# Gated feed-forward with gate and up columns in every chunk and the weights stationary

## The chip, the cores and the metric

One core of a Trainium2 chip runs the whole program. The metric is the device time of one launch in microseconds (us).

## The reference, cut to what matters

A token block of 256 rows with 1024 features goes through ten sublayers of two models, one behind the other. Four of them are gated feed-forwards (before and after each of the two mixers of the first model):

```python
def swiglu(x, w_gu, w_down):
    g, u = jnp.split(x @ w_gu, 2, axis=-1)
    return (jax.nn.silu(g) * u) @ w_down
...
x = layer_norm(ALPHA * x + 0.5 * swiglu(x, ffn_w_gu[l, 0], ffn_w_down[l, 0]), ln_g[l, 0], ln_b[l, 0])
```

`w_gu` is 1024 x 5632 (2816 gate columns, then 2816 up columns) and `w_down` 2816 x 1024, all float32. The second model has two feed-forwards without a gate, `square(relu(h @ w_up)) @ w_down`, with `w_up` 1024 x 4096.

## The kernel before, in words

**Stages and linears.** The program is a list of ten stages, and each is written once for each engine. A gated feed-forward is a stage of kind `ffn1` (four of them: the first, the third, the fourth and the sixth stage), an ungated one `ffn2`. A `Linear` is cut into chunks of CH = 512 output columns, and a chunk into blocks of 256 rows of the contraction (two tiles of 128). The up linear of `ffn1` has 11 chunks of 4 blocks, the down linear 2 chunks of 11 blocks.

**Weights.** SP loads each block (512 KB) into one of 8 `raw` slots (L621). Products are made of float32 numbers split into a high and a low part: ACT copies the block to `whi` (L744, in `split`), DVE subtracts and writes `wlo` (L1285, in `rest`), into one of 4 slots. A slot is free for block b when PE has used block b - 4 (`block_used`).

**Two forms of product.** In the token form (`rows`, L2264 to L2266) the input's tile of 128 tokens is stationary and 512 weight columns stream past it: 3 matmuls of 512 columns for each contraction tile and each half of the tokens, 48 for a chunk. The result has tokens on the partitions. In the paired form (`paired`, L2451, L2452 and L2454) a tile of 128 x 128 weights is stationary; the input's high and low parts lie side by side, so the high weights take one matmul of 512 columns and the low weights one of 256. A chunk has 32 of each, and its result has features on the partitions. It fills all four `stream` banks, each of which holds two halves that must still be added: ACT copies the first half (`copy_halves`, L765), DVE adds the second (`add_halves`, L1296). The token form fills two banks, so that it alternates between two pairs. Paired chunks were in use for chunks 1 to 7 of `ffn2` and for five chunks of each `hg` mixer.

**The gated stage.** All 11 chunks of the up linear are in the token form. Chunks 0 to 4 are gate columns, which ACT evicts with Silu to `silu_gate` (L755); chunk 5 is half gate, half up; chunks 6 to 10 are up columns, which ACT copies to `up_part`. DVE multiplies (`product`, L1534). The down linear needs h with its features on the partitions, so that PE turns h by 44 transposes in a stage (`h_turn`, L2311, first argument `const`): 4 behind chunk 6, 8 behind each of chunks 7 to 10 and 8 inside the down linear. Each turned bank is split by ACT (`hhi`, L792) and DVE (`hlo`, L1321).

**What sets the order.** Each engine runs its own list in program order; they meet at semaphores alone. `evicted` tells PE that `stream` banks are free. A paired chunk starts with the banks that the chunk before did not use last, and waits for the other two ahead of its third output tile:

```python
if at.like - 1 not in lin.paired:
    order = [(j, m) for half in ((0, 1), (2, 3)) for j in range(SPLIT - 2) for m in half]
...
if (j, m) == (0, 2):
    pe.wait_ge(evicted, 2 * lin.chunk(at))
```

The first condition holds for the first paired chunk of a linear: it does eight pairs of matmuls before it needs the other banks, where the later ones do four. Chunk 0 is done by `first_rows` in the later stages (L2293 to L2302) and by `rows` in the first.

## Time and profile before

| | |
|---|---|
| median of 3 runs | 1906.47 us (1905.2 to 1908.08) |
| profiled execution | 1904.79 us, its span 1903.0 us |
| PE busy | 1873.5 us, 98% |
| DVE busy | 1291.4 us, 68% |
| ACT busy | 972.5 us, 51% |
| moved by the DMA queues | 342.47 MB, 180 GB/s |

Matmul records overlap, so that the cost of one is read from the distance between starts and not from its duration. A row of a timeline has the start, the duration, the engine, the line and the operation; "x8" merges eight records, and brackets tell idle time before it and who ended that. PE is TensorE, PEld its weight loads, ACT ScalarE, DVE VectorE.

### The profile page before, as it was taken

What the parts mean: (1) busy time and instruction counts of PE and PEld (TensorE: products, weight loads), DVE (VectorE), ACT (ScalarE), POOL (GpSimd) and SP (SyncE); (2) the same over time, 40 slices, a digit from 0 to 9 for tenths busy, and PEclk for the clock granted to TensorE, in tenths of its full rate; (3) what the DMA queues carried; (4) which work ended last, traced back from release to release, by engine and by line L of the source; (5) the groups of instructions that cost most, each with busy time, mean ns of one, the idle gap of its engine ahead of it and who ended that gap; (6) DMA issues with size and microseconds to landing.
All of it is one profiled execution on the core that took longest, in us unless ns stands there. A gap on an engine that the chain in (4) does not pass through costs nothing.

```text
span 1903.0 us, 25523 instructions
## 1 busy us (share of the span) xinstructions
PE 1873.5 (98%) x9697; PEld 1592.3 (84%) x9697; DVE 1291.4 (68%) x1670; ACT 972.5 (51%) x1266; POOL 36.0 (2%) x67
## 2 busy tenths in 40 slices
PE   9999989999999999999989999999999999999998
PEld 7888877888888888788879888888888988888887
DVE  4565877465646678845576997687656798777754
ACT  5454564454445456545446446455544644555543
POOL 1010100000000000000000000000000000000000
PEclk9999999999999999999999999999999999999999
DMA  9666536665666665576545554466565554455662
GB/s 319 192 197 217 193 110 191 189 183 182 209 191 184 181 186 145 164 216 184 185 146 183 183 181 129 139 197 187 190 192 185 183 173 162 131 172 182 188 196 81
DMA packets 173578, 342.47 MB, mean 180 GB/s; under 512 B 10976, under 2 KB 11152, under 8 KB 173344
## 3 DMA queue, kind: packets, MB, share of 16 engines
q1 hardware_dynamic: 169360, 327.26, 55.3%
q0 software_dynamic: 4112, 13.77, 2.2%
q8 instruction: 70, 1.15, 0.2%
q14 instruction: 36, 0.29, 0.0%
HBM read 338.36 MB, written 1.05 MB: 178 GB/s over the span
## 4 chain that ended last, share of the span: by engine, by line
PE 82%; DVE 14%; ACT 2%; issue 1%; DMA 0%; SPq 0%; DVEq 0%; ACTq 0%
PE stream L2264 18%; PE stream L2266 17%; PE stream L2265 17%; PE stream L2451 6%; DVE wlo L1285 4%; PE stream L2452 3%; PE aux L2311 3%; PE stream L2431 2%; PE stream L2433 2%; PE stream L2432 2%; PE stream L2302 1%; PE stream L2293 1%; PE stream L2294 1%; PE stream L2370 1%; PE stream L2371 1%
## 5 line engine op out<-in xcount | busy, mean ns | idle before, releaser
L1285 DVE TENSOR_TENSOR wlo<-raw,whi 128x1024 fp32r<-128x1024 f32 x584 | 706.4, 1223 | 480.3 <-ACT whi L744 477.6
L744 ACT ACTIVATE whi<-raw 128x1024 fp32r<-128x1024 f32 x584 | 609.3, 1057 | 534.9 <-PE stream L2266 426.1
L2264 PE MATMUL stream<-whi,x_split 128*128 128x512 f32 x944 | 372.7, 395 | 2.7 <-DVE wlo L1285 2.7
L2266 PE MATMUL stream<-whi,x_split 128*128 128x512 f32 x944 | 368.1, 390 | 0.0
L2265 PE MATMUL stream<-wlo,x_split 128*128 128x512 f32 x944 | 367.5, 389 | 0.0
L2264 PE MATMUL stream<-whi,hhi 128*128 128x512 f32 x672 | 263.3, 392 | 0.0
L2266 PE MATMUL stream<-whi,hlo 128*128 128x512 f32 x672 | 261.6, 389 | 0.0
L2265 PE MATMUL stream<-wlo,hhi 128*128 128x512 f32 x672 | 261.5, 389 | 0.0
L2451 PE MATMUL stream<-x_split,whi 128*128 128x512 f32 x672 | 241.0, 398 | 0.0
L2264 PEld LDWEIGHTS stream<-whi,x_split 128*128 128x128 f32 x944 | 177.3, 188 | 38.4 <-issue 3.3
L2266 PEld LDWEIGHTS stream<-whi,x_split 128*128 128x128 f32 x944 | 177.2, 188 | 37.7
L2265 PEld LDWEIGHTS stream<-wlo,x_split 128*128 128x128 f32 x944 | 177.5, 188 | 35.3
L2452 PE MATMUL stream<-x_split,wlo 128*128 128x256 f32 x768 | 199.2, 280 | 0.0
L2452 PEld LDWEIGHTS stream<-x_split,wlo 128*128 128x128 f32 x768 | 144.7, 188 | 8.3
L2451 PEld LDWEIGHTS stream<-x_split,whi 128*128 128x128 f32 x672 | 126.3, 188 | 26.6 <-ACT relu_part L755 0.4
L2266 PEld LDWEIGHTS stream<-whi,hlo 128*128 128x128 f32 x672 | 126.1, 188 | 26.4
L2265 PEld LDWEIGHTS stream<-wlo,hhi 128*128 128x128 f32 x672 | 126.2, 188 | 25.5
L2264 PEld LDWEIGHTS stream<-whi,hhi 128*128 128x128 f32 x672 | 126.2, 188 | 25.4
L2431 PE MATMUL stream<-x_split,whi 128*128 128x256 f32 x416 | 118.8, 286 | 0.0
L2432 PE MATMUL stream<-x_split,whi 128*128 128x256 f32 x416 | 117.7, 283 | 0.0
L2433 PE MATMUL stream<-x_split,wlo 128*128 128x256 f32 x416 | 117.7, 283 | 0.0
L2432 PEld LDWEIGHTS stream<-x_split,whi 128*128 128x128 f32 x416 | 79.8, 192 | 0.3
(345 smaller groups left out, 2091.0 us busy)
## 6 DMA issues: line engine op xcount, KB each, us to landing
raw<-ffn_w_gu SPq DMA_DIRECT2D x176, 512.0 KB, 4.3
raw<-w_in SPq DMA_DIRECT2D x136, 512.0 KB, 4.6
raw<-ffn_w_down SPq DMA_DIRECT2D x88, 512.0 KB, 3.8
raw<-w_up SPq DMA_DIRECT2D x64, 512.0 KB, 4.3
raw<-w_down SPq DMA_DIRECT2D x64, 512.0 KB, 4.4
raw<-c_w_in SPq DMA_DIRECT2D x24, 512.0 KB, 3.8
raw<-ab_w_in SPq DMA_DIRECT2D x20, 512.0 KB, 5.2
raw<-w_out SPq DMA_DIRECT2D x16, 512.0 KB, 3.7
```

The costliest lines, as they stand in the source:

```text
L744: act.activation(split_slots(lin, at, j)[0], raw[:, b % RAW], ACT.Copy).then_inc(hi_ready, 1)
L1285: dve.tensor_tensor(lo, raw[:, b % RAW], hi.bitcast(F32), ALU.subtract).then_inc(lo_ready, 1)
L2264: pe.matmul(bank[tt][:], hi, wh, start=kt == 0, stop=False)
L2265: pe.matmul(bank[tt][:], hi, wl, start=False, stop=False)
L2266: mm = pe.matmul(bank[tt][:], lo, wh, start=False, stop=kt == last)
L2293: pe.matmul(bank[:], hi, wh[:, k], start=(j, k) == (0, 0), stop=False)
L2311: t = pe.transpose(bank[:, m * P:(m + 1) * P], src[:, bass.ds(first + m * P, P)], ident)
L2431: pe.matmul(to, wh, xhi[:, kt, tokens], start=first, stop=False, skip_group_check=True)
L2432: pe.matmul(to, wh, xlo[:, kt, tokens], start=False, stop=False, skip_group_check=True)
L2433: mm = pe.matmul(to, wl, xhi[:, kt, tokens], start=False, stop=last, skip_group_check=True)
L2451: pe.matmul(banks[m], wh[:, k], both, start=kt == 0, stop=False)
L2452: mm = pe.matmul(banks[m][:, S:CH], wl[:, k], xhi[:, kt], start=False, stop=False)
```

## The change

Every chunk c of the up linear now holds gate columns 256c to 256c + 255 and the up columns of the same numbers, so that each is whole: its h can be made at once. A block comes by two transfers of 256 KB, whose rows are 1 KB and not 2 KB (`transfers`). Chunk 0 stays in the token form, chunks 1 to 10 become paired. Output tiles 0 and 1 of a chunk are the gate, 2 and 3 the up half. For each paired chunk ACT applies Silu in place in `h_part` (`gate`), DVE multiplies (`product`), and ACT and DVE split the product straight into `hhi` and `hlo` (`h_hi`, `h_lo`), with no transpose. Only the h of chunk 0 is turned, by 4 transposes into one bank behind chunk 1. The arrays `silu_gate`, `up_part` and `relu_part` give way to two buffers `h_part`, which `ffn2` uses too.

```diff
@@ -164,7 +162,7 @@
         for i in range(2):
-            up = Linear(io["ffn_w_gu"][l, i], D, 2 * D_FF)
+            up = Linear(io["ffn_w_gu"][l, i], D, 2 * D_FF, paired=range(1, 11), sides=2)
             down = Linear(io["ffn_w_down"][l, i], D_FF, D)
...
@@ -270,6 +268,15 @@
         return self.w[j * BK * P:(j + 1) * BK * P, self.columns(at)]
+
+    def transfers(self, slot, at, j):
+
+        if self.sides == 1:
+            return [(slot, self.source(at, j).rearrange("(k p) n -> p k n", p=P))]
+        n, rows = CH // self.sides, slice(j * BK * P, (j + 1) * BK * P)
+        return [(slot[:, :, i * n:(i + 1) * n],
+                 self.w[rows, bass.ds(at.c * n + i * self.w.shape[1] // self.sides, n)]
+                 .rearrange("(k p) n -> p k n", p=P)) for i in range(self.sides)]
 
     def columns(self, at):
         return bass.ds((self.order[at.like] if at.like < len(self.order) else at.c) * CH, CH)
...
@@ -350,10 +357,7 @@
 
-        silu_gate = sb("silu_gate", [P, TT, FF1], at=56 * KB)
-        up_part = [sb(f"up_part{i}", [P, TT, CH], at=56 * KB + TT * FF1 * 4 + i * 4 * KB) for i in range(2)]
-
-        relu_part = [sb(f"relu_part{i}", [P, TT, CH], at=(64 + 4 * i) * KB) for i in range(2)]
...
@@ -552,6 +561,11 @@
 
+        transfers_of = [lin.sides for lin in lins for _ in range(lin.n * lin.kb)]
+
+        def landed(b):
+            return 16 * sum(transfers_of[b % RAW:b + 1:RAW])
+
...
@@ -617,8 +631,8 @@
-                    src = lin.source(at, j)
-                    sp.dma_start(raw[:, slot], src.rearrange("(k p) n -> p k n", p=P)).then_inc(raw_in[slot], 16)
+                    for to, src in lin.transfers(raw[:, slot], at, j):
+                        sp.dma_start(to, src).then_inc(raw_in[slot], 16)
...
@@ -886,36 +900,56 @@
 
             def ffn1(st):
                 up, down = st.lins
-                split(up, At(0), SPLIT)
+                h0, l0 = seen.h, gated_before(st)
+                a0 = seen.aux
 
                 def gate(at):
-                    split(up, At(at.like + 1, at.turn))
-                    evict(up, at, lambda tt: silu_gate[:, tt, bass.ds(at.c * CH, CH)], ACT.Silu)
-
-                chunks(act, 0, 5, gate, peel=1)
-                split(up, At(6))
-                act.wait_ge(block_used, up.done(At(5)))
+
+                    act.wait_ge(evicted, 2 * up.chunk(at) + 2)
+                    tiles = part_tiles(at)(0, 2)
+                    act.activation(tiles, tiles, ACT.Silu).then_inc(gate_made, 1)
+
+                def h_hi(at):
+
+                    act.wait_ge(h_made, h0 + at.c + 1)
+                    act.activation(hhi[:, bass.ds(2 * at.c, 2), :], part_tiles(at)(0, 2), ACT.Copy).then_inc(gated_hi, 1)
+
+                def body(at, to=up):
+
+                    before = At(at.like - 1, at.turn)
+                    split(up, at, 2, 3)
+                    gate(before)
+                    split(up, at, 3, 4)
+                    h_hi(before)
+                    split(to, At(at.like + 1, at.turn) if to is up else At(0), 0, 2)
+                    if at.like > 2:
+
+                        act.wait_ge(gated_lo, l0 + at.c - 2)
+                    copy_halves(up, at, part_tiles(at))
+
+                split(up, At(1))
+                act.wait_ge(block_used, up.done(At(0)))
                 for tt in range(TT):
-                    bank = stream[up.banks(At(5)) + tt]
-                    act.activation(silu_gate[:, tt, 5 * CH:FF1], bank[:, 0:CH // 2], ACT.Silu)
-                    act.activation(up_part[1][:, tt, CH // 2:CH], bank[:, CH // 2:CH], ACT.Copy).then_inc(evicted, 1)
-                h0 = seen.h
-                for c in range(6, up.n):
-                    if c + 1 < up.n:
-                        split(up, At(c + 1))
-                    else:
-                        ahead(down)
-                    if c > 6:
-
-                        act.wait_ge(h_made, h0 + c - 6)
-                    evict(up, At(c), lambda tt: up_part[c % 2][:, tt, :])
-                    if c == PARAMS_CHUNK and st is stages[0]:
-                        seen.aux += 1
-                    h_turn_hi(*FF1_TILES[c - 1])
+                    bank = stream[up.banks(At(0)) + tt]
+                    act.activation(h_part[0][:, tt, 0:S], bank[:, 0:S], ACT.Silu)
+                    act.activation(h_part[0][:, tt, S:CH], bank[:, S:CH], ACT.Copy).then_inc(evicted, 1)
+                split(up, At(2), 0, 2)
+                copy_halves(up, At(1), part_tiles(At(1)))
+                turn_hi(by_tokens(hhi), 4)
+
+                act.wait_ge(aux_full, a0 + 1)
+                body(At(2))
+                chunks(act, 3, up.n - 1, body)
+                if st is stages[0]:
+                    seen.aux += 1
+                body(At(up.n - 1), down)
+                split(down, At(0), 2, 3)
+                gate(At(up.n - 1))
+                split(down, At(0), 3, 4)
+                h_hi(At(up.n - 1))
                 split(down, At(0), SPLIT, SPLIT + 2)
-                h_turn_hi(*FF1_TILES[up.n - 1])
                 last_layer(down, SPLIT + 2)
-                seen.h += 6
+                seen.h = h0 + up.n
...
@@ -1522,31 +1556,49 @@
 
                 up, down = st.lins
-                chunks(dve, 1, 7, lambda at: rest(up, at), peel=1)
-
-                def product(c):
-
-                    cols = slice(CH // 2, CH) if c == 5 else slice(0, CH)
-                    at = c * CH + cols.start - FF1
-                    dve.wait_ge(evicted, 2 * (up.c0 + c) + 2)
-                    part = silu_gate[:, :, at:at + cols.stop - cols.start]
-                    dve.tensor_tensor(part, part, up_part[c % 2][:, :, cols], ALU.mult).then_inc(h_made, 1)
-
-                product(5)
-                for c in range(6, up.n):
-                    if c + 1 < up.n:
-                        rest(up, At(c + 1))
-                    else:
-                        ahead(down)
-                    product(c)
-                    if c == PARAMS_CHUNK and st is stages[0]:
-                        copy_params()
-
-                        dve.wait_ge(const_in, 32)
-                    h_turn_lo(*FF1_TILES[c - 1])
+                l0 = gated_before(st)
+
+                def product(at):
+
+                    dve.wait_ge(gate_made, l0 + at.c)
+                    part = part_tiles(at)
+                    dve.tensor_tensor(part(0, 2), part(0, 2), part(2, 4), ALU.mult).then_inc(h_made, 1)
+
+                def h_lo(at):
+
+                    dve.wait_ge(gated_hi, l0 + at.c)
+                    tiles = bass.ds(2 * at.c, 2)
+                    dve.tensor_tensor(hlo[:, tiles, :], part_tiles(at)(0, 2), hhi[:, tiles, :].bitcast(F32),
+                                      ALU.subtract).then_inc(gated_lo, 1)
+
+                def body(at, to=up):
+
+                    before = At(at.like - 1, at.turn)
+                    rest(up, at, 2, 3)
+                    product(before)
+                    rest(up, at, 3, 4)
+                    h_lo(before)
+                    rest(to, At(at.like + 1, at.turn) if to is up else At(0), 0, 2)
+                    add_halves(up, at, part_tiles(at))
+
+                rest(up, At(1))
+                dve.wait_ge(evicted, 2 * up.c0 + 2)
+                part = h_part[0][:]
+                dve.tensor_tensor(part[:, :, 0:S], part[:, :, 0:S], part[:, :, S:CH], ALU.mult).then_inc(h_made, 1)
+                rest(up, At(2), 0, 2)
+                add_halves(up, At(1), part_tiles(At(1)))
+                turn_lo(by_tokens(hhi), by_tokens(hlo), 4)
+                chunks(dve, 2, up.n - 1, body)
+                if st is stages[0]:
+                    copy_params()
+
+                    dve.wait_ge(const_in, 32)
+                body(At(up.n - 1), down)
+                rest(down, At(0), 2, 3)
+                product(At(up.n - 1))
+                rest(down, At(0), 3, 4)
+                h_lo(At(up.n - 1))
                 rest(down, At(0), SPLIT, SPLIT + 2)
-                h_turn_lo(*FF1_TILES[up.n - 1])
                 last_layer(st, SPLIT + 2)
...
@@ -2512,18 +2558,21 @@
                     first_rows(up)
                 else:
                     rows(up, At(0), xhi, xlo, ready=x_ready())
-                chunks(pe, 1, 7, lambda at: rows(up, at, xhi, xlo), peel=1)
-                h0 = seen.h
-                a0 = seen.aux + (st is stages[0])
-                for c in range(6, up.n):
-                    if c > 6:
-                        rows(up, At(c), xhi, xlo)
-                    if c == PARAMS_CHUNK and st is stages[0]:
-                        turn_params()
-                    h_turn(c - 1, h0)
-                last_layer(st, hhi, hlo, ready=lambda j, tt: (aux_free, a0 + 2 + 2 * ((j + 1) // 2)),
-                           hook=lambda j: h_turn(up.n - 1, h0) if j == 2 else None)
-                seen.h += 6
+                paired(up, At(1))
+                h0, a0, l0 = seen.h, seen.aux, gated_before(st)
+                pe.wait_ge(h_made, h0 + 1)
+                bank = aux_bank()
+                for a in range(2):
+                    for tt in range(TT):
+                        t = pe.transpose(bank[:, (2 * a + tt) * P:(2 * a + tt + 1) * P],
+                                         h_part[0][:, tt, a * P:(a + 1) * P], ident)
+                t.then_inc(aux_full, 1)
+                chunks(pe, 2, up.n - 1, lambda at: paired(up, at))
+                if st is stages[0]:
+                    turn_params()
+                paired(up, At(up.n - 1))
+                last_layer(st, hhi, hlo, ready=lambda j, tt: (gated_lo, l0 + j) if j else (aux_free, a0 + 1))
+                seen.h = h0 + up.n
```

**ACT, chunk 0 and what comes behind it.** In the rows below, from ACT's list in the first gated stage, `h_part_69` and `h_part_70` are the two buffers of `h_part`. Before:

```order
L744 ACTIVATE whi<-raw 128x1024 [waits block_used,raw_in7]
L755 ACT_TABLE_LOAD
L755 ACTIVATE silu_gate<-stream 128x512 [waits block_used]
L755 ACTIVATE silu_gate<-stream 128x512
L246 UNCONDITIONAL_BRANCH
```

Now:

```order
L758 ACTIVATE whi<-raw 128x1024 [waits block_used,raw_in7]
L934 ACT_TABLE_LOAD
L934 ACTIVATE h_part_69<-stream 128x256 [waits block_used]
L935 ACTIVATE h_part_69<-stream 128x256
L934 ACTIVATE h_part_69<-stream 128x256
L935 ACTIVATE h_part_69<-stream 128x256
L758 ACTIVATE whi<-raw 128x1024 [waits block_used,raw_in0]
L758 ACTIVATE whi<-raw 128x1024 [waits block_used,raw_in1]
L779 ACTIVATE h_part_70<-stream 128x512 [waits tiles_full]
```

The eviction of chunk 0 is four instructions in place of two, behind the same table load and the same four splits of chunk 1.

**PE, from chunk 0 to its eviction's wait.** Before, chunk 1 was in the token form in the two free banks, and the first instruction that waited for the eviction of chunk 0 stood at the start of chunk 2:

```order
L2265 MATMUL stream<-wlo,x_split 128x512
L2266 MATMUL stream<-whi,x_split 128x512
L246 UNCONDITIONAL_BRANCH
L246 ISA
L2256 ISA [waits evicted]
L2264 MATMUL stream<-whi,x_split 128x512 [waits lo_ready]
```

Now, inside chunk 1 (the first row with a wait is the ninth of its pairs of matmuls):

```order
L2498 MATMUL stream<-x_split,wlo 128x256
L2497 MATMUL stream<-x_split,whi 128x512 [waits evicted]
L2498 MATMUL stream<-x_split,wlo 128x256
L2497 MATMUL stream<-x_split,whi 128x512
L2498 MATMUL stream<-x_split,wlo 128x256
```

The wait has moved up by a chunk less eight pairs.

**ACT, a late chunk of the first gated stage.** Before, while PE did chunk 6:

```order
L744 ACTIVATE whi<-raw 128x1024 [waits block_used,raw_in7]
L755 ACTIVATE up_part_70<-stream 128x512 [waits block_used]
L755 ACTIVATE up_part_70<-stream 128x512
L792 ACTIVATE hhi<-aux 128x2x128 [waits aux_full] x2
L744 ACTIVATE whi<-raw 128x1024 [waits block_used,raw_in0]
```

Now, chunk 9 (`L779` is `copy_halves`, `L910` the gate and `L915` `h_hi` of the chunk before):

```order
L758 ACTIVATE whi<-raw 128x1024 [waits block_used,raw_in6]
L910 ACTIVATE h_part_69<-h_part_69 128x512 [waits evicted]
L758 ACTIVATE whi<-raw 128x1024 [waits block_used,raw_in7]
L915 ACTIVATE hhi<-h_part_69 128x512 [waits h_made]
L758 ACTIVATE whi<-raw 128x1024 [waits block_used,raw_in0]
L758 ACTIVATE whi<-raw 128x1024 [waits block_used,raw_in1]
L779 ACTIVATE h_part_70<-stream 128x512 [waits tiles_full,gated_lo]
L779 ACTIVATE h_part_70<-stream 128x256 [waits tiles_full]
L779 ACTIVATE h_part_70<-stream 128x256 [waits block_used]
```

Silu and the high part of h, each of 512 elements, now stand between the splits.

## Rows read from the trace of the kernel before

**Rows 1.** Page, busy time of the engines and the granted clock.
```profile
PE 1873.5 (98%) x9697; PEld 1592.3 (84%) x9697; DVE 1291.4 (68%) x1670; ACT 972.5 (51%) x1266; POOL 36.0 (2%) x67
...
PEclk9999999999999999999999999999999999999999
```

**Rows 2.** Waits of PE, the matmul that waited longest.
```profile
PE stream L2264 <- DVE wlo L1285: 2.7, 2, 2.5
```

**Rows 3.** Groups by line and shape: busy us, mean ns | idle before.
```profile
L2264 PE MATMUL stream<-whi,x_split 128*128 128x512 f32 x944 | 372.7, 395 | 2.7 <-DVE wlo L1285 2.7
...
L2452 PE MATMUL stream<-x_split,wlo 128*128 128x256 f32 x768 | 199.2, 280 | 0.0
...
L2311 PE MATMUL aux<-const,silu_gate 128*128 128x128 f32 x176 | 23.2, 273 | 0.0
```

**Rows 4.** Timeline of ACT, second gated stage (start us, us, what).
```profile
328.49 1.07 ACT L755 ACTIVATE silu_gate<-stream 128x512 f32 x2
...
339.37 1.07 ACT L755 ACTIVATE silu_gate<-stream 128x512 f32 x2
...
417.88 1.07 ACT L755 ACTIVATE up_part<-stream 128x512 f32<-128x512 f32 x2
...
429.65 1.07 ACT L755 ACTIVATE up_part<-stream 128x512 f32<-128x512 f32 x2
```

**Rows 5.** Timeline of PE, second gated stage, ends of its chunks 1 to 10.
```profile
316.44 0.39 PE L2264 MATMUL stream<-whi,x_split 128*128 128x512 f32 x1
...
429.22 0.47 PE L2264 MATMUL stream<-whi,hhi 128*128 128x512 f32 x1
```

**Rows 6.** Timeline of PE, the first stage with paired chunks alone.
```profile
1274.88 0.39 PE L2451 MATMUL stream<-x_split,whi 128*128 128x512 f32 x1
...
1277.72 0.49 PE L2451 MATMUL stream<-x_split,whi 128*128 128x512 f32 x1
...
1286.21 1.04 PE L2311 MATMUL aux<-const,relu_part 128*128 128x128 f32 x8
...
1354.61 0.40 PE L2264 MATMUL stream<-whi,hhi 128*128 128x512 f32 x1
```

**Rows 7.** Timelines of ACT, DVE and PE in that stage.
```profile
1276.60 1.07 ACT L755 ACTIVATE relu_part<-stream 128x512 f32<-128x512 f32 x2
...
1309.72 0.38 ACT L765 ACTIVATE relu_part<-stream 128x256 f32<-128x256 f32 x1 [1.03 <-PE stream L2454]
...
1320.99 0.38 ACT L765 ACTIVATE relu_part<-stream 128x256 f32<-128x256 f32 x1 [1.03 <-PE stream L2454]
...
1310.14 0.42 DVE L1296 TENSOR_TENSOR relu_part<-stream,relu_part 128x256 f32<-128x256 f32 x1 [0.98 <-ACT relu_part L765]
...
1310.93 0.40 PE L2451 MATMUL stream<-x_split,whi 128*128 128x512 f32 x1
```

**Rows 8.** Timeline of ACT and PE, chunk 0 of gated stages 2 and 1.
```profile
318.28 1.28 ACT L755 ACT_TABLE_LOAD   x1
...
319.57 1.09 ACT L755 ACTIVATE silu_gate<-stream 128x512 f32<-128x512 f32 x2
...
22.96 1.28 ACT L755 ACT_TABLE_LOAD   x1
...
24.25 1.09 ACT L755 ACTIVATE silu_gate<-stream 128x512 f32<-128x512 f32 x2
...
21.62 0.39 PE L2264 MATMUL stream<-whi,x_split 128*128 128x512 f32 x1
```

**Rows 9.** Timeline of ACT, two evictions of 256 columns each.
```profile
383.91 0.66 ACT L792 ACTIVATE hhi<-aux 128x256 fp32r<-128x256 f32 x2
```

**Rows 10.** DMA queues of the page, and a window of the first stage.
```profile
q1 hardware_dynamic: 169360, 327.26, 55.3%
...
q0 software_dynamic: 4112, 13.77, 2.2%
...
20.00:86.00 66.00, 66.00 (x293) 54.62 (x293) 30.49 (x26) 32.92 (x40) 0.00 (x0) 1.00 0.76 237
```

More of the change, by code:

```diff
@@ L40 @@
 RAW = 8
-PARAMS_CHUNK = 8
 SPLIT = 4
@@ L112 @@
 FF1 = D_FF
-FF1_TILES = {5: (0, 2)} | {c: (2 + 4 * (c - 6), 4) for c in range(6, 11)}
 PARAM_ROWS = 64
@@ L254, with __init__ @@
 class Linear:
-    def __init__(self, w, k, n, order=(), walk=None, paired=()):
-        self.order, self.walk, self.paired = order, walk, paired
+    def __init__(self, w, k, n, order=(), walk=None, paired=(), sides=1):
+        self.order, self.walk, self.paired, self.sides = order, walk, paired, sides
         self.w, self.kb, self.n = w, k // (P * BK), n // CH
@@ L351, in program @@
         hlo = sb("hlo", [P, 32, S], F32R, at=32 * KB)
-        silu_gate = sb("silu_gate", [P, TT, FF1], at=56 * KB)
-        up_part = [sb(f"up_part{i}", [P, TT, CH], at=56 * KB + TT * FF1 * 4 + i * 4 * KB) for i in range(2)]
-        relu_part = [sb(f"relu_part{i}", [P, TT, CH], at=(64 + 4 * i) * KB) for i in range(2)]
+        h_part = [sb(f"h_part{i}", [P, TT, CH], at=(64 + 4 * i) * KB) for i in range(2)]
         y = sb("y", [P, TT, D], at=72 * KB)
@@ L446, in program @@
         tiles_from = lambda dst, first: lambda a, b: dst[:, first + a:first + b, :]
-        relu_tiles = lambda at: lambda a, b: relu_part[at.like % 2][:].rearrange("p a (b t) -> p (a b) t", b=2)[:, a:b]
+        part_tiles = lambda at: lambda a, b: h_part[at.like % 2][:].rearrange("p a (b t) -> p (a b) t", b=2)[:, a:b]
+        by_tokens = lambda t: t[:, 0:2].rearrange("p a (h t) -> p (a h) t", h=2)
+        gated_before = lambda st: (st.lins[0].n - 1) * [s for s in stages if s.kind == "ffn1"].index(st)
         raw_in = [sem(f"raw_in{i}") for i in range(RAW)]
@@ L1211, in halves @@
                 def halves(at):
-                    copy_halves(up, at, relu_tiles(at))
+                    copy_halves(up, at, part_tiles(at))
                 def h_hi(at):
@@ L1217, in h_hi @@
                     act.activation(hhi[:, bass.ds(4 * at.c, 4), :],
-                                   relu_part[at.like % 2][:].rearrange("p a (b t) -> p (a b) t", b=2), ACT.Copy)\
+                                   h_part[at.like % 2][:].rearrange("p a (b t) -> p (a b) t", b=2), ACT.Copy)\
                         .then_inc(h_hi_ready, 1)
@@ L1222, in ffn2 @@
                 split(up, At(1))
-                evict(up, At(0), lambda i: relu_part[0][:, i, :], ACT.Relu)
+                evict(up, At(0), lambda i: h_part[0][:, i, :], ACT.Relu)
                 split(up, At(2), 0, 2)
@@ L2163, in square @@
                     dve.wait_ge(evicted, 2 * up.chunk(at) + 2)
-                    part = relu_part[at.like % 2][:]
+                    part = h_part[at.like % 2][:]
                     dve.scalar_tensor_tensor(part, part, 0.0, part, ALU.max, ALU.mult).then_inc(h_made, 1)
@@ L2395, in walked @@
                 seen.x_src, seen.x_early = [src], True
-            def h_turn(c, h0):
-                first_tile, tiles = FF1_TILES[c]
-                pe.wait_ge(h_made, h0 + c - 4)
-                for tt in range(TT):
-                    turn(silu_gate[:, tt], first_tile * P, tiles)
             def columns(lin, at, ready=None, hook=None):
@@ L2827, in ffn2 @@
                 for tt in range(TT):
-                    turn(relu_part[0][:, tt], 0, 4)
+                    turn(h_part[0][:, tt], 0, 4)
                 chunks(pe, 2, up.n, lambda at: paired(up, at))
```

16 lines of the change are left out of this document (9 added, 7 removed).

## The prediction

> **What bounds the kernel now.** I read the page first: PE is busy 98% of the span, and its granted clock is full in all forty slices, the 2.4 GHz level [rows 1]. Then the waits of PE: the longest total for a `stream` matmul is 2.7 us in 1903 [rows 2]. So the sum of what PE issues is the time, and ACT, DVE and the DMA queues count only where they make PE wait. Then the groups, for the shapes [rows 3], and the timelines, for distances between starts, since a record of a matmul lasts longer than what it costs. I compare the gated stages as they are with the first `ffn2` stage, which is the only place where nothing but paired chunks run one behind the other.
>
> **PE in a gated stage now.** ACT evicts at the end of each chunk, so its evictions tell the period of a chunk: 339.37 - 328.49 = 10.88 us for a token chunk without a turn, and 429.65 - 417.88 = 11.77 us with 8 transposes [rows 4]. A turn of 8 costs 0.89 us, 0.11 us for each, and one of 4 half of it, 0.45 us. From the start of chunk 1 to the end of chunk 10 and its turn it is 429.22 - 316.44 = 112.78 us [rows 5], which agrees with 10 x 10.88 + 0.45 + 4 x 0.89 = 112.8. The last turn, in the down linear, adds 0.89. Together 113.67 us a stage.
>
> **PE in a gated stage after it.** Chunk 1 is the first paired one: 1286.21 - 1274.88 = 11.33 us [rows 6], with a pause of 0.1 us inside. Chunks 2 to 7 with a turn of 8 take 1354.61 - 1286.21 = 68.40 us [rows 6]; here the turn has 4 transposes, so that 0.45 goes off: 67.95. Chunks 8 to 10 take 1320.99 - 1309.72 = 11.27 us each [rows 7], 33.81. The sum is 113.09 us: 0.58 less than 113.67. In four stages **-2.3 us**. So 40 fewer transposes give 4.5 us a stage, and ten chunks that cost 0.39 us more each give 3.9 of it back. Both forms stream 24576 columns for a chunk (48 x 512, or 32 x 512 + 32 x 256), but the paired form needs 64 matmuls and weight loads for what the token form does with 48.
>
> Here a rule of the Trainium skill would say otherwise. The page "TensorE: Matmul & The Clock Gate" (Wait — 56ns, not 53.3ns?) puts a warm matmul at its columns over 2.4 GHz plus a fixed 2.5 ns or so. By it, as an estimate, sixteen more matmuls cost a chunk 0.04 us and not 0.39, and the change would give some 16 us more. The trace doesn't agree: 48 matmuls take 10.88 us, 227 ns each, and the page's sum would be 10.4 us.
>
> **The wait that is added.** Chunk 1 needs the banks of chunk 0 at its ninth pair. In `ffn2` PE comes to it 1277.72 - 1274.88 = 2.84 us behind the start of chunk 1 [rows 6]; there ACT began the eviction 1276.60 - 1274.88 = 1.72 us behind that start and took 1.07 [rows 7], so it ended at 2.79: just in time. In a gated stage ACT must first load the table that has Silu. That load starts when the splits of chunk 1 are done, at 318.28, and the eviction at 319.57 [rows 8]: 3.13 us behind the start of chunk 1 at 316.44 [rows 5]. Today nobody waits for it, since chunk 1 has banks of its own. The eviction is then four instructions of 256 columns; two such take 0.66 us [rows 9], one 0.385 (the third `copy_halves` shows 0.38 [rows 7]), so each further one adds 0.275: 0.385 + 3 x 0.275 = 1.21 us. End at 4.34, 1.55 us later than in `ffn2`, where PE was just held. PE stands still for some 1.55 us in each of the three later gated stages, 4.65 us. In the first stage chunk 1 starts at 21.62 and the eviction at 24.25 [rows 8], 2.63 us behind; with 1.21 that is 3.84, 1.05 us more than 2.79. Together **+5.7 us**. Bounds: 0, if PE's order had more slack than in `ffn2`, and 4 x 1.28 more, if the table load repeated.
>
> A second rule speaks against the change. The page "ScalarE: Activation LUTs" (What ACT_TABLE_LOAD costs) adds a drain of about 1.38 us to a table load of 1.28. With it, as an estimate, the four pauses would cost 5.5 us more. The rows show the load from 318.28 to 319.56 and the eviction at 319.57, so no drain stands there, and the sum goes by the rows.
>
> **The start.** Blocks come by two transfers with rows of half the size. The trace has no packets of 1 KB in number. Queue 1 moved 169360 packets in 55.3% of 16 engines' span, 99 ns for each of 1.93 KB; queue 0 moved 4112 in 2.2%, 163 ns for each of 3.35 KB [rows 10]. The difference is 45 ns a KB and leaves 12 ns for a packet whatever its size. An engine has 16 packets more in a block, 0.2 us. PE's second block waits for the landing of the first two, **+0.4 us** once (0 if bytes alone count, 3.2 us if a packet of 1 KB costs 99 ns). Later it is covered: the queues are busy 0.76 in the heaviest stretch of the first stage [rows 10], and 12 ns on 99 make it 0.85. SP issues twice as much, with eight blocks of lead.
>
> **What is hidden.** ACT's splits, copies, Silu and high part make about 7 us in a chunk of 11.27, and DVE's four blocks of 1.22, the product, the low part and the adds about 8. The tightest meeting is that of the third add with the fifth pair of the next chunk: in `ffn2` the add ends at 1310.14 + 0.42 = 1310.56 and PE comes at 1310.93 [rows 7], 0.37 us later. Silu and `h_hi` stand behind this add in ACT's list, and in both lists between splits that PE needs 5.6 us on, so they are costed at nothing. If one came ahead of it, PE would wait in each chunk.
>
> **The sum.** -2.3 + 5.7 + 0.4 = +3.8 us on the profiled execution's 1904.79 us, or 1908.6. The median of the runs is 1.7 us above that execution, so that I put the median after at 1906.47 + 3.8 = **1910.3 us**. Something like 0.2% (3.8 us) is what a measurement of this kernel can tell from no change, and the forecast lies on that line.
>
> **Rivals.**
> - *Each pair runs at its quicker rate.* Behind the turn in `ffn2` chunk 2 took 68.40 - 0.89 - 5 x 11.27 = 11.16 us, 0.11 less than its followers. If all nine and chunk 1 had that or somewhat better (0.16), 5 us go: 1905. Against it: all five later chunks of `ffn2` took 11.27. Chance 0.13.
> - *PE isn't held in chunk 1*, if the eviction ends in time after all: 1910.3 - 5.7 = 1904.6. For it only that ffn2's margin is not seen exactly. Chance 0.08.
> - *A matmul costs its columns*, half a 512-column one for 256, so that a pair takes 340 ns and a chunk 10.88 us: 40 x 0.39 = 15.6 us less, 1895, a faster kernel. The fixed 2.5 ns of the Trainium skill's page on TensorE would lead there. Against it: 32 pairs in 11.27 us are 352 ns. Chance 0.04.
> - *The other side: a wait in every chunk.* `copy_halves` or its add comes a split late (1.06 us on ACT), because ACT or DVE is held by the new exchange of Silu, product and the two parts of h. It decides from 0.37 us of delay on; 1.06 - 0.37 = 0.69 us in 36 chunks is 25 us: 1935. Against it: each piece of the exchange has 2 us or more before PE's next need. Chance 0.08.
> - *The queues become the bound*, if a packet of 1 KB costs as one of 2 KB: 0.76 would become 1.5, more than there is, and the up linears would take half as long again. Chance 0.02.
>
> **How the numbers follow.** The forecast has 0.65, with a range of its own from 1908 to 1913, about half of it on either side of the line. Faster by over 0.2%: the column case and a little of the rest, 0.07. Within: half of the forecast and the two mild rivals, 0.49. Slower: the other half and the two severe cases, 0.44. The range of 1904 to 1916 leaves out the column case, the severe ones and a small edge.
>
> **What would show it.** Right: chunks 3 to 10 at 11.27 us by ACT's third copies; a PE pause of 1.5 us inside chunk 1 of three stages, 1 us in the first, ended by ACT's line 935; 16 transposes of h in all; no drain behind the table load; the first stage's second block landing some 0.4 us later. Wrong: a pause of PE in the steady chunks, a chunk nearer 10.9 or 11.1, or DMA as the releaser of ACT's splits in the up linear.

## The result, and the profile after

The changed kernel takes 1911.93 us (median of 7 runs, 1910.67 to 1918.22) against 1905.90 (7 runs, 1905.2 to 1908.08): a ratio of 1.0031, 95% interval 1.0021 to 1.0041. It is slower by some 6.0 us. 1910.3 was forecast.

The profiled execution took 1912.12 us with a span of 1910.5, 7.5 more than the span before. The page of the changed kernel, busy time by engine, the granted clock and the first queue:

```profile
PE 1873.3 (98%) x10177; PEld 1608.8 (84%) x10177; DVE 1349.9 (71%) x1806; ACT 1002.3 (52%) x1342; POOL 35.8 (2%) x67
PEclk9999999999999999999999999999999999999999
q1 hardware_dynamic: 217232, 327.27, 54.2%
```

PE is the bound as before [rows 1]. Queue 1 moves the same bytes in 47872 more packets, and its share of the span did not rise (55.3% before, [rows 10]). The waits of PE (line, releaser; us in total, times, longest):

```profile
PE stream L2497 <- ACT h_part L935: 5.7, 4, 1.4
PE stream L2316 <- DVE wlo L1319: 4.2, 1, 4.2
```

The first row is new: four pauses, one in each gated stage, ended by the eviction of chunk 0. The second answers to [rows 2], where it was 2.7 us: the wait for the very first block.

The second gated stage on PE: the start of chunk 1, the last two matmuls ahead of the pause and the first behind it, the turn of 4, and the start of the down linear:

```profile
320.79 0.39 PE L2497 MATMUL stream<-x_split,whi 128*128 128x512 f32 x1
...
323.25 0.40 PE L2497 MATMUL stream<-x_split,whi 128*128 128x512 f32 x1
323.48 0.28 PE L2498 MATMUL stream<-x_split,wlo 128*128 128x256 f32 x1
325.18 0.50 PE L2497 MATMUL stream<-x_split,whi 128*128 128x512 f32 x1 [1.42 <-ACT h_part L935]
...
333.73 0.60 PE L2567 MATMUL aux<-const,h_part 128*128 128x128 f32 x4
...
435.66 0.40 PE L2316 MATMUL stream<-whi,hhi 128*128 128x512 f32 x1
```

From 320.79 to 435.66 it is 114.87 us, where 113.67 were worked out for the stage before (1.20 more; 0.97 more was forecast). The third stage has 114.84 and the fourth 114.85, read the same way, the first 115.23. In the 113.67 the last turn, which stood inside the down linear, is an estimate of 0.89. Reading on to the end of the down linear, where PE begins to turn the next x, needs no estimate. Before, then now:

```profile
489.41 0.60 PE L2311 MATMUL aux<-const,x 128*128 128x128 f32 x4
```

```profile
494.83 0.60 PE L2363 MATMUL aux<-const,x 128*128 128x128 f32 x4
```

It was 489.41 - 316.44 = 172.97 us and is 494.83 - 320.79 = 174.04, 1.07 more (the last turn was worth 1.02 and not 0.89). The other stages, read the same way, have 1.04, 1.05 and 1.01 more. Four stages give 4.2 of the 7.5 us.

ACT in the same place, the splits of chunk 1, the table load and the four evictions:

```profile
320.59 2.01 ACT L758 ACTIVATE whi<-raw 128x1024 fp32r<-128x1024 f32 x2 [0.71 <-PE stream L2354]
322.62 1.28 ACT L934 ACT_TABLE_LOAD   x1
323.91 0.38 ACT L934 ACTIVATE h_part<-stream 128x256 f32<-128x256 f32 x1
324.19 0.38 ACT L935 ACTIVATE h_part<-stream 128x256 f32<-128x256 f32 x1
324.46 0.39 ACT L934 ACTIVATE h_part<-stream 128x256 f32<-128x256 f32 x1
324.72 0.41 ACT L935 ACTIVATE h_part<-stream 128x256 f32<-128x256 f32 x1
```

The last eviction ends at 325.13, which is 4.34 us behind the start of chunk 1: the forecast's number to the hundredth.

Another 3.0 us come at the start of the kernel, and some 0.3 in the mixer between the first two gated stages. ACT's first splits, and those of chunk 1 in the first stage with what follows:

```profile
8.66 1.06 ACT L758 ACTIVATE whi<-raw 128x1024 fp32r<-128x1024 f32 x1 [2.41 <-DMA raw<-ffn_w_gu]
...
11.50 1.06 ACT L758 ACTIVATE whi<-raw 128x1024 fp32r<-128x1024 f32 x1 [1.30 <-DMA raw<-ffn_w_gu]
...
25.33 1.06 ACT L758 ACTIVATE whi<-raw 128x1024 fp32r<-128x1024 f32 x1 [2.14 <-DMA raw<-ffn_w_gu]
26.41 1.28 ACT L934 ACT_TABLE_LOAD   x1
27.70 0.38 ACT L934 ACTIVATE h_part<-stream 128x256 f32<-128x256 f32 x1
```

In the kernel before, the first two splits began at 6.87 and 9.55. Here PE stood still until 11.12 and came to chunk 1 at 24.59, not at 21.62. The windows of the changed kernel, then of the one before (stretch; length; busy us of PE, PEld, DVE, ACT, POOL; granted clock; DMA share; GB/s):

```profile
11.10:13.60 2.50, 2.48 (x6) 1.84 (x7) 1.49 (x2) 1.06 (x1) 0.00 (x0) 0.55 1.10 350
13.60:15.00 1.40, 1.40 (x10) 1.39 (x8) 0.22 (x1) 0.30 (x1) 0.23 (x1) 0.58 1.11 350
15.00:22.00 7.00, 7.00 (x34) 5.82 (x32) 6.05 (x6) 4.87 (x6) 4.50 (x9) 1.00 1.08 385
```

```profile
11.00:15.00 4.00, 3.82 (x21) 3.13 (x20) 3.65 (x5) 2.98 (x4) 2.47 (x5) 1.00 1.06 389
15.00:22.00 7.00, 7.00 (x32) 5.79 (x32) 4.54 (x4) 3.30 (x4) 2.27 (x5) 1.00 1.04 413
```

Two things are to be seen. The DMA engines are full in both kernels (shares over 1.0), and with half rows they carry 350 GB/s where 389 went before. And behind the idle 4.2 us the granted clock fell to 0.55, about the lower of the two levels: six 512-column matmuls took 2.49 us, 0.42 each in place of 0.23. PE's first matmul on block 0 came 1.78 us later than before (11.12 against 9.34), and chunk 1 2.97 us later (24.59 against 21.62): the low clock added the other 1.2 us. This execution was late for more than its transfers: four kernels below have the same transfers in the same order of issue, and their first split begins at 7.34 to 7.71 us, not at 8.66. What made it a microsecond later here isn't shown.

### The profile page after: what moved, and what is told of

Its sections match the earlier page's. It is cut to its first block, busy times and chain, and to the rows that moved or that the text cites. A ratio compares the mean times of both kernels' runs of the same rounds, so it can differ in the third digit from the quotient of the medians.

```text
span 1910.5 us, 27556 instructions
## 1 busy us (share of the span) xinstructions
PE 1873.3 (98%) x10177; PEld 1608.8 (84%) x10177; DVE 1349.9 (71%) x1806; ACT 1002.3 (52%) x1342; POOL 35.8 (2%) x67
## 3 DMA queue, kind: packets, MB, share of 16 engines
q1 hardware_dynamic: 217232, 327.27, 54.2%
HBM read 338.36 MB, written 1.05 MB: 178 GB/s over the span
## 4 chain that ended last, share of the span: by engine, by line
PE 80%; DVE 14%; ACT 3%; issue 1%; DMA 1%; SPq 1%; DVEq 0%; ACTq 0%
PE stream L2497 19%; PE stream L2498 11%; PE stream L2316 10%; PE stream L2318 10%; PE stream L2317 10%; DVE wlo L1319 4%; PE stream L2500 3%; PE stream L2477 2%; PE stream L2479 2%; PE stream L2478 2%; PE aux L2363 2%; PE stream L2354 1%; PE stream L2345 1%; PE stream L2422 1%; PE stream L2346 1%
## 5 line engine op out<-in xcount | busy, mean ns | idle before, releaser
L2497 PE MATMUL stream<-x_split,whi 128*128 128x512 f32 x1792 | 643.4, 398 | 5.7 <-ACT h_part L935 5.7
L2498 PE MATMUL stream<-x_split,wlo 128*128 128x256 f32 x2048 | 532.4, 280 | 0.0
L2498 PEld LDWEIGHTS stream<-x_split,wlo 128*128 128x128 f32 x2048 | 386.2, 189 | 22.6
L2497 PEld LDWEIGHTS stream<-x_split,whi 128*128 128x128 f32 x1792 | 336.9, 188 | 77.7 <-ACT h_part L935 6.9
L1330 DVE TENSOR_TENSOR h_part<-stream,h_part 128x512 f32<-128x512 f32 x162 | 83.2, 514 | 125.7 <-ACT h_part L779 125.7
L779 ACT ACTIVATE h_part<-stream 128x512 f32<-128x512 f32 x162 | 73.7, 455 | 180.6 <-PE stream L2500 180.6
L2316 PE MATMUL stream<-whi,x_split 128*128 128x512 f32 x304 | 122.5, 403 | 4.2 <-DVE wlo L1319 4.2
L2318 PE MATMUL stream<-whi,x_split 128*128 128x512 f32 x304 | 119.3, 392 | 0.0
L2317 PE MATMUL stream<-wlo,x_split 128*128 128x512 f32 x304 | 118.9, 391 | 0.0
L2479 PE MATMUL stream<-x_split,wlo 128*128 128x256 f32 x416 | 117.7, 283 | 0.0
L2500 PE MATMUL stream<-x_split,whi 128*128 128x512 f32 x256 | 101.8, 398 | 0.0
L2478 PEld LDWEIGHTS stream<-x_split,whi 128*128 128x128 f32 x416 | 79.8, 192 | 0.3
```

Of the source, the lines that this page charges most:

```text
L1330: a = dve.tensor_tensor(to, second, to, ALU.add)
L2316: pe.matmul(bank[tt][:], hi, wh, start=kt == 0, stop=False)
L2317: pe.matmul(bank[tt][:], hi, wl, start=False, stop=False)
L2318: mm = pe.matmul(bank[tt][:], lo, wh, start=False, stop=kt == last)
L2478: pe.matmul(to, wh, xlo[:, kt, tokens], start=False, stop=False, skip_group_check=True)
L2479: mm = pe.matmul(to, wl, xhi[:, kt, tokens], start=False, stop=last, skip_group_check=True)
```

## The experiments

The theory after the result: (a) the four pauses are ACT's order and table load; (b) the trade of transposes against dearer chunks is as the rows told; (c) the rest is the two transfers with 1 KB rows, and only at the start. Rivals: the transfers cost in every stage; the dearer chunk has another cause than the count of matmuls.

### The two transfers alone, in the kernel before

Each block of `w_gu` comes by two transfers. In the first kernel they take one contraction tile each, with rows of 2 KB; in the second they take half the columns each, with rows of 1 KB.

```diff
-sp.dma_start(raw[:, slot], src.rearrange("(k p) n -> p k n", p=P)).then_inc(raw_in[slot], 16)
+src = src.rearrange("(k p) n -> p k n", p=P)
+# first kernel:  (raw[:, slot, i:i+1], src[:, i:i+1]) for i in 0, 1
+# second kernel: (raw[:, slot, :, i*256:(i+1)*256], src[:, :, i*256:(i+1)*256]) for i in 0, 1
... (the counts that ACT waits for follow)
```

> The kernel before, with each block of the gated up linears loaded by two transfers of 256 KB whose rows keep their 2 KB (split by contraction tile). Theory A, the late start of the change comes from its rows of 1 KB: the second block lands within 0.5 us of before (9.55 us) and the time moves by less than 1 us. Theory B, it comes from twice the number of transfers and SP's issues: the second block lands near 11.5 us and the time grows by some 3 us.

> The kernel before, with each block of the gated up linears loaded by two transfers of 256 KB with rows of 1 KB (split by columns), as the change does. Both theories of the start: PE waits some 1.7 us longer for its first weights and later for the second block, the time grows by about 3 us (1.0016), and nothing else moves, since the queues have room later. If it stays at 1906 the start of the change is late for another reason.

Measured: 1907.51 us for 2 KB rows (ratio 1.0007, 0.9998 to 1.0017) and 1907.13 for 1 KB rows (1.0010, 1.0000 to 1.0019), against 1905.81. The 3 us that were expected of the second kernel did not come. The first split began at 7.50 and 7.58 us, against 6.87, the second at 10.15 and 10.37, against 9.55. So having two transfers costs the first block some 0.6 us whatever the rows (the three profiles with one transfer start at 6.25 to 6.87, those with two and the same order of issue at 7.34 or later); neither time can be told from the other. The rows show in the rate, with all else equal. The window of the kernel with 2 KB rows, then of the one with 1 KB rows:

```profile
11.00:15.00 4.00, 3.83 (x22) 3.09 (x21) 3.40 (x4) 3.16 (x5) 1.86 (x4) 1.00 1.05 395
```

```profile
11.00:15.00 4.00, 3.70 (x21) 2.96 (x21) 3.31 (x4) 3.29 (x5) 1.36 (x3) 1.00 1.11 349
```
The 1 KB rows show in one place more, where ACT's last split of chunk 1 in the first stage waits for its block (timeline of ACT, 1 KB rows):

```profile
24.05 1.06 ACT L756 ACTIVATE whi<-raw 128x1024 fp32r<-128x1024 f32 x1 [3.01 <-DMA raw<-ffn_w_gu]
25.13 1.28 ACT L767 ACT_TABLE_LOAD   x1
26.42 1.09 ACT L767 ACTIVATE silu_gate<-stream 128x512 f32<-128x512 f32 x2
```

With 2 KB rows the table load stands at 23.56 and nothing waits. In this kernel nobody needs that eviction soon, so the 1.5 us don't reach PE.

### The transfers taken back, in the kernel after

```diff
-if self.sides == 1:
+if True:
     return [(slot, self.source(at, j).rearrange("(k p) n -> p k n", p=P))]
... (the counts that ACT waits for follow)
```

This kernel leaves out the pairing of gate and up columns: it multiplies columns that don't belong together, and only its time is of use.

> The kernel after, but each block of w_gu comes by one transfer with rows of 2 KB from 512 neighbouring columns, as in the kernel before, so that the columns which are multiplied as gate and up are not those of the reference; all instructions of the engines stay. It undoes the transfers alone. Theory: the two transfers of 1 KB rows cost only at the start of the kernel (block 0 split 1.8 us later; in the profile of after also a granted clock of 0.55 for some 4 us behind it), and the four pauses in chunk 1 of the gated stages have nothing to do with them. Then block 0's split is back at 6.9 us, chunk 1 of the first stage at 21.7, the first stage's pause at 1.05 instead of 1.4, the other pauses stay at 1.4 us each, and the time is before + 4 x 1.2 = 1910.5 us (start cost 1.5 us in the median). Rival: the half rows cost in every stage (0.76 of the DMA engines' time became more, each wait of a split a little later): then the stages too become shorter, 1907 or less, and the pauses with them. Rival 2: the transfers cost nothing in the median: 1911.9.

Measured: 1909.47 us (11 runs) against 1906.39; ratio 1.0018, 1.0009 to 1.0027, some 3.4 us. The first split began at 6.25 us, and PE's waits:

```profile
PE stream L2497 <- ACT h_part L935: 5.2, 4, 1.4
PE stream L2316 <- DVE wlo L1319: 3.0, 2, 1.8
```

The pauses stay, 0.5 us shorter in all, since the first stage's is back at 0.93. What is left is +3.4 us, and the forecast without its term for the start is -2.3 + 5.7 = +3.4. The transfers thus cost 6.0 - 3.4 = 2.6 us; the intervals of the two ratios overlap a little, so the size is loose. That the half rows cost in each stage is refuted by the later stages, which are as long. The second one on PE, chunk 1 and the start of the down linear:

```profile
319.38 0.39 PE L2497 MATMUL stream<-x_split,whi 128*128 128x512 f32 x1
...
434.17 0.40 PE L2316 MATMUL stream<-whi,hhi 128*128 128x512 f32 x1
```

It takes 114.79 us, against 114.87 with half rows, and the third and fourth 114.87 and 114.90, against 114.84 and 114.85. (The busy share of queue 1, 54.2% in both, can't decide this: with 2 KB rows it is 53.6 to 55.3% from one kernel's profile to another's.)

### The count of matmuls

In the kernel before, the low matmul of each token chunk 1 to 10 is made in two halves of 256 columns: 64 matmuls and weight loads in a chunk, for the same columns.

```diff
-pe.matmul(bank[tt][:], hi, wl, start=False, stop=False)
+for cut in (slice(0, S), slice(S, CH)):
+    pe.matmul(bank[tt][:, cut], hi, wl[:, cut], start=False, stop=False)
```

> The kernel before, with each matmul of the low weights in chunks 1 to 10 of the gated up linears done as two of 256 columns: 64 matmuls and weight loads in a chunk instead of 48, columns as before, still the token form. Theory, the paired form costs more because it has more matmuls: a chunk takes 11.27 us instead of 10.88, 40 x 0.39 = 15.6 us more. Rival, the extra cost belongs to the weights being stationary, and a matmul costs its columns and 2.5 ns: 40 x 16 x 2.5 ns = 1.6 us more.

Measured: 1916.01 us; ratio 1.0063, 1.0046 to 1.0080. ACT's evictions tell the period of three chunks without a turn:

```profile
342.43 1.07 ACT L755 ACTIVATE silu_gate<-stream 128x512 f32 x2
...
353.58 1.06 ACT L755 ACTIVATE silu_gate<-stream 128x512 f32 x2
...
364.72 1.07 ACT L755 ACTIVATE silu_gate<-stream 128x512 f32 x2
```

A chunk takes 11.15 us, 0.27 more than 10.88 [rows 4]; 40 of them are 10.8 us, which is about the time that the run shows (10.2). Neither expectation was met: it is two thirds of the 15.6 us and six times the 1.6. So 0.27 of the 0.39 us that a paired chunk costs more is the sixteen more matmuls, 17 ns each, if they cost the same there. A fixed 2.5 ns, as the page "TensorE: Matmul & The Clock Gate" of the Trainium skill has it (Wait — 56ns, not 53.3ns?), would make 0.04; the trace doesn't agree. The other 0.12 us is special to the paired form and stays open.

### The pause, taken apart

Three kernels change ACT's order only: the table loaded early by a Silu of one column ahead of the splits of chunk 0; the eviction of chunk 0 put between splits 0, 1 and splits 2, 3 of chunk 1; and both.

```diff
+if st is stages[0]:
+    act.wait_ge(eps_set, 1)
+act.activation(small[:, 63:64], eps_cols[:, 0:1], ACT.Silu)     # table early
...
-split(up, At(1))
+split(up, At(1), 0, 2)                                          # eviction first
 ... (the four evictions of chunk 0)
+split(up, At(1), 2)
```

> The changed kernel, with the Silu table loaded by a small Silu ahead of chunk 0 of each gated stage and the eviction of chunk 0 placed between the splits of chunk 1 (two before, two behind). Theory, PE's pauses in chunk 1 are the table load and the two splits ahead of the eviction: all four pauses (5.7 us) go, chunk 1 takes 11.3 us and the time falls by 5.5 to 6.5 us below the change, to about 1906. Rival, the pause comes from something else that PE or ACT waits for there (the DMA of the blocks, the slots): it stays over 0.5 us each.

> The kernel after with one change: a Silu of one column ahead of the splits of chunk 0 of the gated up linear loads the table early; the order of splits and evictions stays. Theory: each pause of 1.4 us is the table load of 1.28 us between the last split of chunk 1 and the eviction of chunk 0, plus four evictions instead of two. Without the load 0.1 to 0.3 us of pause is left: 4 x 1.28 = 5.1 us less than after, 1906.8. Rival: the pause is made of the two late splits alone, or of the slow start: 1911 to 1912.

> The kernel after with one change: chunk 0 is evicted between splits 0, 1 and splits 2, 3 of chunk 1; the table is still loaded right ahead of the first eviction. Theory: the eviction now starts with PE's start of chunk 1, load 1.28 and evictions 1.1 us end 2.5 us behind it, 0.3 us ahead of PE's need at 2.8: no pause in the later three stages, the splits 2 and 3 come 2.4 us later but still ahead of PE. 4 x 1.4 = 5.6 us less than after, 1906.3. Rival: the splits 2 and 3 of chunk 1 come too late and a wait for them takes the place of the one removed: some 1 us in each stage, 1910.

Measured: both 1905.60 (ratio to before 1.0002, 0.9992 to 1.0011); the table alone 1906.11 (1.0002, 0.9993 to 1.0011); the order alone 1905.48 (0.9991, 0.9982 to 1.0000). No wait of PE for `h_part` stands in any of the three lists of waits. ACT with the order alone, second stage:

```profile
316.06 2.01 ACT L758 ACTIVATE whi<-raw 128x1024 fp32r<-128x1024 f32 x2 [1.77 <-PE stream L2355]
318.08 1.28 ACT L934 ACT_TABLE_LOAD   x1
319.38 0.38 ACT L934 ACTIVATE h_part<-stream 128x256 f32<-128x256 f32 x1
```

The load now begins 0.89 us before PE starts chunk 1 (318.97), the last eviction ends at 320.60, and PE comes to these banks at 321.78. Either half of the cause taken away is enough, as the pause was 1.4 us long and each half gives 1.3 or more; they don't add. With the table early PE resumes 0.15 us late (320.78 where its neighbours' distance says 320.63), the rest that the expectation named. Each way takes 5.8 to 6.5 us off the changed kernel's median; theory (a) is shown. The rival, that splits 2 and 3 would now come late, is refuted: PE has no wait for them.

These kernels also show what the trade alone is worth. The second stage with both edits, from chunk 1 to the end of the down linear:

```profile
316.49 0.39 PE L2501 MATMUL stream<-x_split,whi 128*128 128x512 f32 x1
...
488.86 0.60 PE L2367 MATMUL aux<-const,x 128*128 128x128 f32 x4
```

That is 172.37 us against 172.97 before, 0.60 less; the four stages together have 2.5 less.

### The start

On top of both edits, the first tile of x is issued from ACT's queue, which puts SP's first weight block 0.45 us earlier. Then more of the matmuls on ones that the kernel already does there (`busy`) fill PE's wait for block 0, in this version and in the changed kernel as it was.

```diff
-load_x(0)                                   # SP
+act.dma_start(x[:, 0], io["x"][0, 0:P]).then_inc(x_in[0], 16)
...
-busy(2)
+busy(8)       # the changed kernel;  busy(5) in the other
```

> The version with both changes to ACT's order (table early, eviction of chunk 0 between the splits), and the first tile of x issued from ACT's queue, so that SP issues block 0 of the weights 0.45 us earlier. Theory: the start of the kernel is bound by the landing of block 0 (7.34 us in the profile of the version without this) and block 1 (10.12): block 0 lands at 6.9 or so, PE's wait for it falls from 2.4 to 2.0 us, 0.4 us less in all: 1905.2, a little below the kernel before at 1905.8. Rival: the bytes ahead of block 0 in the DMA engines bind, not the issue: no change, 1905.6. Rival 2: the transfers from two queues disturb each other and x comes later: PE turns x later, 1906 or more.

> The version with the table early, the eviction of chunk 0 between the splits and x issued from ACT's queue once more, to stand beside the others of this call and to see whether its 1904.1 us against 1906.4 holds: ratio 0.9990 with an interval that leaves out 1, or 0.9998 (the version without x from ACT had 1.0002).

> The version with the table early, the eviction of chunk 0 between the splits and x issued from ACT's queue, and three more rounds of the matmuls on ones: PE is busy until 8.9 us, where the first matmul on block 0 starts at 9.12. Theory: with 1.7 us of idle time the clock there did not fall in the profile, so little is left to win: 1904.0, at most 0.3 us below the version without. Rival: some executions have the drop: 0.5 to 1 us less. Rival 2: the rounds delay block 0's matmuls: 1905.

> The kernel after with six more rounds of the matmuls on ones (busy(8) for busy(2)) while PE waits for block 0 of the first stage. In the profile of after PE stood still 4.2 us there and its granted clock was 0.55 to 0.58 from 11.1 to 15 us, where 6 matmuls of 512 columns took 0.43 us each and not 0.23; that cost some 1.7 us on top of the later landing. Theory: the idle time is what drops the clock. Each round takes 0.5 us, so PE is busy until 10.0 us and idle for 1.1 only: the clock stays at 1.00 and the median, in which some executions have the drop, falls by 0.5 to 1.5 us: 1910.4 to 1911.4. Rival: the drop has another cause (it also stands at 270 to 290 and 980 to 1000 us in some profiles), then nothing changes: 1911.9. Rival 2: the matmuls on ones delay the first real one: more than 1912.

Measured: x from ACT 1904.11 us against 1906.39 (ratio 0.9990, 0.9981 to 0.9999), and once more 1903.78 against 1905.64 (0.9991, 0.9982 to 1.0000); with the filling 1903.70 (0.9990, 0.9981 to 0.9999). The first split begins at 6.67 and 6.90 us. This is the best version found, about 1.9 us below the kernel before: a gain seen in three runs of it, though within the 0.2% that I called no change. In its second profile chunk 1 starts at 21.62 as before the change, and the span is 1900.5 us, 2.5 less than 1903.0: what the four stages give. The filling adds nothing that can be told.

Filling alone in the changed kernel gave nothing: 1913.03 us (5 runs, ratio 1.0037, 1.0023 to 1.0050). At the start it did what was expected, its clock is 1.00 there. But the time saved is gone behind it. ACT, PE and the windows of this kernel:

```profile
23.96 1.06 ACT L758 ACTIVATE whi<-raw 128x1024 fp32r<-128x1024 f32 x1 [3.10 <-DMA raw<-ffn_w_gu]
25.04 1.28 ACT L934 ACT_TABLE_LOAD   x1
```

```profile
27.60 0.50 PE L2497 MATMUL stream<-x_split,whi 128*128 128x512 f32 x1 [2.36 <-ACT h_part L935]
```

```profile
15.00:24.00 9.00, 9.00 (x43) 7.52 (x42) 5.10 (x5) 3.22 (x4) 3.19 (x7) 1.00 1.06 383
24.00:26.00 2.00, 1.23 (x8) 0.82 (x6) 0.95 (x1) 1.98 (x2) 0.00 (x0) 1.00 1.13 294
26.00:28.00 2.00, 0.40 (x2) 0.36 (x3) 0.70 (x2) 1.53 (x5) 0.00 (x0) 1.00 1.10 364
28.00:30.00 2.00, 2.00 (x9) 1.76 (x8) 0.27 (x1) 0.03 (x1) 0.00 (x0) 0.60 1.10 348
30.00:34.00 4.00, 4.00 (x19) 3.44 (x19) 1.82 (x2) 2.09 (x2) 0.00 (x0) 0.77 1.11 348
```

PE comes to chunk 1 at 22.26, 2.33 us earlier than in the changed kernel, but ACT's last split begins only 1.37 earlier, at 23.96, since it waits for the eighth block (with 1 KB rows in the kernel before it was 24.05). This split holds the table load and the eviction, and PE's pause grows from 1.4 to 2.4 us. It ends at 27.60, where it ended at 25.93 with whole rows. The low clock comes back too, now behind this pause, and costs 1.6 us up to the turn (37.68 - 27.60 = 10.08 us, 8.51 in the changed kernel). So the first stage is bound by the landing of its first eight blocks as long as the eviction of chunk 0 stands behind the last split; where it stands ahead, the same late block holds nobody.

## Why the prediction was right, and where it was off

- **PE is the bound, and the trade of 40 transposes against ten dearer chunks.** Right. From the turn of chunk 1 to the down linear it is 435.66 - 333.73 = 101.93 us, where 67.95 + 33.81 = 101.76 were forecast. The steady period is the forecast's 11.27 by ACT's third copies (46.59 and 57.88 in the first stage: 11.29). The term of -2.3 us stands, at 2.5 in the profile of the kernel with both edits. Its span is still only 0.3 below the one before: chunk 1 starts 0.61 later (22.23), and a stretch of low clock at 732 to 736 us, which the profile before doesn't have, costs 1.5 (730.94 to 740.63 is 9.69, the same work was 8.15). Why the medians of these kernels only equal the one before is not shown beyond that. The prediction's estimate of "some 16 us more" is miscounted: 40 x (0.39 - 0.04) is 14 us.
- **The pause.** Right in place, releaser, number and size: chunk 1 with its pause takes 333.73 - 320.79 = 12.94 us against 11.33 in `ffn2`, 1.61 more, where 1.55 was forecast. The length owes something to luck: without a pause the chunk takes 11.27 in the kernel with both edits, so that each pause costs PE 1.67 and the four 6.6 us, 0.9 more than forecast. No drain stands behind the table load (322.62 + 1.28, then 323.91), so the 1.38 us of the Trainium skill ("ScalarE: Activation LUTs", What ACT_TABLE_LOAD costs) is not in this time.
- **The first stage's pause** was forecast at 1.05 us and took 1.4 in the profile, since the last split of chunk 1 waited 2.14 us for its block. Without half rows it is 0.93.
- **The start.** This is the term that was mis-sized: +0.4 us, against 2.6 by the runs with and without the half rows, and 3.0 in the profiled execution (1.8 of it a later block 0, 1.2 low clock). The step that failed is the sentence "Later it is covered: the queues are busy 0.76 in the heaviest stretch of the first stage". That window was 66 us long. Short windows of the same trace show full engines from 4 us to 32 us, the first 12 us of that window among them:

```profile
4.00:8.00 4.00, 2.80 (x15) 1.91 (x13) 0.73 (x2) 1.72 (x3) 0.00 (x0) 1.00 1.01 371
...
28.00:32.00 4.00, 4.00 (x19) 3.34 (x18) 2.15 (x2) 1.38 (x2) 0.00 (x0) 1.00 1.06 389
```

  There more time for each byte delays every block down to the eighth, and the eighth holds the eviction that PE waits for. The price of a packet was about right: 16 engines at a share of 1.10 with 350 GB/s make 51 ns for 1 KB (the forecast's 12 + 45 = 57; the busy share that went into it differs by 1.7 points between profiles, so it was not a sharp number). The second transfer also costs 0.6 us at the first block, which the forecast did not have. The upper bound of 3.2 us held. The forecast's own signs told it: ACT's second split came 1.95 us later (11.50 against 9.55) and not 0.4, and DMA was the releaser of a split in chunk 1, which it had named as a sign of being wrong.
- **The range** held because the bounds of the start were in it. The rivals were all refuted: PE is held, the pair rate is 11.27, a matmul doesn't cost its columns, and no steady chunk has a wait.

Together: -2.3 + 5.7 + 2.6 = +6.0 us. This closes by its making, since the 2.6 is what the kernel with whole rows left over. The profiled execution can be added up by itself: 6.6 for the pauses less 2.5 for the trade is 4.2 in the four stages (rounded), with 3.0 at the start and 0.3 in the mixer 7.5 us. So the forecast's 3.4 for the stages was 0.8 too low, and that the runs with whole rows gave 3.4 again is in part luck.

## What to carry to other kernels

- A share of queue time must be read in windows as short as the buffering is deep. The first eight blocks here ran at full DMA share, and an average over 66 us hid it.
- Where banks are shared, the eviction belongs ahead of work on the same engine that isn't urgent, and a table load ahead of both. Either alone took a pause of 1.4 us away.
- Before trading transposes for more and narrower matmuls, price the matmul count: it ate most of the gain here (of 4.5 us a stage, the dearer chunks took 3.9 back).

## What was not expected of the hardware

- Two matmuls of 256 columns, each with its weight load, cost 17 ns more than one of 512 (0.27 us for sixteen such pairs in a chunk).
- The granted clock falls behind some of PE's idle times and not behind others of like length. Behind 4.2 us at the start of the changed kernel it was 0.55. Behind 2.73 us in the kernel with the table early it fell too, behind 2.83 us in the one with the order alone it didn't:

```profile
11.00:15.00 4.00, 4.00 (x19) 3.20 (x19) 1.99 (x3) 1.97 (x4) 1.20 (x2) 0.74 1.10 349
```

```profile
11.00:15.00 4.00, 3.69 (x21) 3.00 (x20) 3.20 (x4) 3.30 (x5) 1.22 (x3) 1.00 1.10 348
```

  Such stretches also stand near 270 to 290 us in six of the thirteen profiles, near 730 to 745 in four, and near 980 to 1000 in all. They cost up to 2 us (1.5 in the kernel with both edits), and a single execution's span is uncertain by that much: the kernel with whole rows had a profiled span of 1912.1 us with four of them, though its median is 2.5 us below that of the changed kernel. The page's row of 40 slices hides them: it has 9 everywhere for the kernel before, whose clock is 0.50 from 982 to 988 us. What decides whether the clock falls stays open.
- Rows of half the size cost the full DMA engines 10% of their rate (350 against 389 GB/s). In the later gated stages, where the engines are not full, they cost no time: the stages are equal within 0.1 us.
